# A second token tile's mixer work moved behind the first expert scores in a two-block fp32 kernel

## The chip, the cores and the metric

One core of one Trainium2 chip runs the whole program. The metric is the device time of one execution in microseconds (us). All data are fp32. The core has a matrix engine (TensorE, PE in the rows), a vector engine (VectorE, DVE), a scalar engine (ScalarE, ACT), GpSimd (POOL) and a sync engine (SP). SP issues plain DMAs on the hardware queue q1; POOL issues the gathers of expert rows on the software queue q0. Both queues run on the same 16 DMA engines.

## What is computed

Two blocks run one after the other on 256 tokens of width 1024. The change lies in the second, from the end of its mixer to the expert layer:

```python
o_hg = _rmsnorm_2(o, gn_w) * gate                 # linear attention, 4 heads of 128
y = jax.nn.gelu(y, approximate=False)             # state-space part
y = y * jax.nn.sigmoid(y @ w_glu + b_glu)         # "GLU"
mixed = jnp.concatenate([o_hg, o_s5], axis=-1) @ w_out[l]
x = x + gt1 * mixed
h2 = _rmsnorm_2(x, norm_ffn_w[l]) * (1.0 + sc2) + sh2
# _peer, per block of 128 tokens:
qh = (hb @ w_q).reshape(tb, PEER_HEADS, 2, PEER_HALF)          # 8 heads
s1, s2 = qh[:, :, 0] @ keys1.T, qh[:, :, 1] @ keys2.T          # 128 keys each
v1, i1 = lax.top_k(s1, 16); v2, i2 = lax.top_k(s2, 16)
best, pos = lax.top_k(v1[..., :, None] + v2[..., None, :], 16) # eidx from pos, i1, i2
gates = jax.nn.softmax(best)
act = jax.nn.gelu(jnp.einsum('td,thkd->thk', hb, u_tab[eidx]))
return jnp.einsum('thk,thkd->td', gates * act, v_tab[eidx])
```

After it comes `x + gt2 * peer` and a last RMSNorm. Each token picks 16 of 16,384 experts for each of 8 heads, and an expert has a row of 1024 in each of two tables.

## The kernel before

Tokens stand as two tiles of 128 (t = 0, 1). `mixer` (from L3119) holds the block's mixer, `projection_and_experts` (from L3607) what follows it; both write one program for each engine, run in order and tied by semaphores. No scheduler moves anything.

**End of the mixer.** PE reads the attention states of both tiles (L3373, L3380; `hg_out` counts tiles), multiplies the GLU weights by all 256 tokens (L3236, through `features(10, ...)`), turns the heads (L3395). ACT squares, roots and opens the GLU gate (L3595 to L3600), DVE scales the heads (L3523 to L3536), POOL multiplies by the gate (L3216).

**Output projection.** `out_tile(t, tile, k0, k1)` (L4084) multiplies one of 8 output tiles, `added` (L3946) adds the residual, `out_square` and `out_sum` (L4003, L4091) collect the norm, `inverted`, `out_root`, `out_scale`, `out_shift` (L3951, L4007, L3958, L4011) apply it.

**Queries and scores.** `PEER_QUERIES` lists 13 query steps: heads 0 to 4 for tile 0, heads 5 to 7 for both tiles, heads 0 to 4 for tile 1. `query_product` (L4107) multiplies a head's 1 MB of `peer_wq` by the tokens, `score` (L4124) the queries by the keys. `Search` (from L3667) finds the 16 experts on DVE; for the first unit (tile 0, head 0), `opening` (L3702) gives the first 8 and then the other 8, each told by `ranked`.

**Experts.** For each of 256 experts e (2 tiles, 8 heads, 16 each), POOL gathers 128 rows of 8 KB (L3848), one for each token: 1 MB. DVE takes the dot product (L3883), ACT makes a diagonal weight (L4042 to L4048), PE adds the weighted second half (L4186, `expert_done`). The ring has 8 buffers; gather e waits for expert e - 8. Buffers 4 to 7 lie in the weight ring and wait for the output products of tile 1 (`out_product`). Between experts PE does queries and scores of later heads. The weights of heads 0 and 1 are loaded by `early_loads`, of 2, 3, 5, 6, 4 and 7 by `sync`; a head waits for its whole group in `PEER_LOADS` = (0), (1), (2), (3, 5, 6, 4), (7).

## Time and profile before

| | us |
|---|---|
| median of 3 runs | 3091.54 (3090.03 to 3092.69) |
| profiled execution | 3085.72 |
| its span | 3083.9 |
| busy in the span: PE, DVE, ACT, POOL | 2921.8, 1841.9, 820.7, 575.8 |

A line of a timeline gives the start and the time of one or more instructions in us from the span's start, the engine, the line of the kernel, what is written from what, and the count; in brackets stands how long the engine was idle before it, and what ended that.
### The profile page before, as it was taken

Reading aid. Unit: us, or ns where it says so; the run is one execution under the profiler, and the core shown is the slowest. Engines: PE = TensorE matmul, PEld = TensorE weight load, DVE = VectorE, ACT = ScalarE, POOL = GpSimd, SP = SyncE. Lnnn points to the kernel's source line nnn. Section 1 sums busy time; section 2 is a strip of 40 time slices with the busy share of each in tenths; the row PEclk is TensorE's granted clock in tenths of the full one; section 3 lists DMA queues with packets and bytes.
Section 4 is the critical chain, followed back from the end, with each engine's and each line's share of the span. In section 5 each row is a group of like instructions: output and inputs, shape, how many; then the busy total and the mean of one; then the engine's idle time right before and its main releaser. Section 6 shows DMA issues by size and latency. Waiting matters only on the chain. (4 is left out here: it accounts for less than half of the span.)

```text
span 3083.9 us, 37671 instructions
## 1 busy us (share of the span) xinstructions
PE 2921.8 (95%) x14204; PEld 2256.3 (73%) x14204; DVE 1841.9 (60%) x3947; ACT 820.7 (27%) x1898; POOL 575.8 (19%) x561
## 2 busy tenths in 40 slices
PE   8999999999999999999999999999999999888777
PEld 3888877758888888887998878888887744443222
DVE  4556675367775677645345557534146677776774
ACT  2132344311002100012223430010033354444443
POOL 2223321010000000103112100000000344344342
PEclk8999999999999999999999999999999999999999
DMA  6212211154342443534222234569433899999997
GB/s 248 90 62 69 69 45 65 42 171 136 123 134 77 153 157 130 174 123 136 98 96 69 83 112 156 195 241 321 159 123 126 320 420 420 420 420 420 419 415 314
DMA packets 278068, 582.23 MB, mean 189 GB/s; under 512 B 11704, under 2 KB 228920, under 8 KB 241536
## 3 DMA queue, kind: packets, MB, share of 16 engines
q0 software_dynamic: 51504, 338.98, 27.6%
q1 hardware_dynamic: 226384, 240.84, 23.6%
q8 instruction: 114, 1.87, 0.2%
q14 instruction: 66, 0.54, 0.1%
HBM read 578.70 MB, written 1.08 MB: 188 GB/s over the span
## 5 line engine op out<-in xcount | busy, mean ns | idle before, releaser
L4186 PE MATMUL banks<-weight_ring,work 128*128 128x512 f32 x512 | 250.8, 614 | 56.7 <-ACT work L4048 55.9
L4186 PE MATMUL banks<-work 128*128 128x512 f32 x512 | 251.0, 613 | 40.1 <-ACT work L4048 36.6
L436 DVE CUSTOM_DVE_ANT_0 work<-work 128x1024 f32<-128x1024 f32 x176 | 210.0, 1227 | 95.0 <-ACT branches L2830 45.5
L2608 PE MATMUL banks<-normed,weight_ring 128*128 128x256 f32 x1088 | 237.1, 381 | 6.7 <-ACT normed L2808 3.8
L2608 PEld LDWEIGHTS banks<-normed,weight_ring 128*128 128x128 f32 x1088 | 207.6, 191 | 35.6 <-ACT normed L2808 4.2
L4186 PEld LDWEIGHTS banks<-weight_ring,work 128*128 128x128 f32 x512 | 88.1, 190 | 167.7 <-ACT work L4048 103.8
L3883 DVE CUSTOM_DVE_ANT_0 weight_ring<-weight_ring,branches 128x1024 f32<-128x1024 f32 x128 | 156.8, 1225 | 83.1 <-DMA weight_ring<-experts,branches 79.8
L3883 DVE CUSTOM_DVE_ANT_0 work<-work,branches 128x1024 f32<-128x1024 f32 x128 | 156.9, 1226 | 79.5 <-DMA work<-experts,branches 74.2
L4186 PEld LDWEIGHTS banks<-work 128*128 128x128 f32 x512 | 87.5, 189 | 153.5 <-ACT work L4048 88.4
L406 POOL DMA_DIRECT2D work<-ada_turned x96 | 51.0, 532 | 769.3 <-DVEq L442 769.3
L3848 POOL DMA_INDIRECT weight_ring<-experts,branches x128 | 138.8, 1084 | 192.3 <-PE banks L4186 187.8
L3848 POOL DMA_INDIRECT work<-experts,branches x128 | 132.9, 1038 | 208.8 <-PE banks L4186 168.9
L1944 PE MATMUL banks<-work 128*128 128x256 f32 x768 | 171.0, 379 | 0.0
L1944 PEld LDWEIGHTS banks<-work 128*128 128x128 f32 x768 | 145.9, 190 | 19.8
L2608 PE MATMUL banks<-branches,weight_ring 128*128 128x256 f32 x736 | 160.0, 379 | 0.0
L2608 PEld LDWEIGHTS banks<-branches,weight_ring 128*128 128x128 f32 x736 | 139.7, 190 | 18.9
L1361 POOL TENSOR_TENSOR branches<-weight_ring 128x512 f32<-128x512 f32 x40 | 51.4, 1284 | 529.7 <-DVE work L1580 142.0
L860 PE MATMUL banks<-normed,weight_ring 128*128 128x256 f32 (+1 forms) x512 | 137.0, 424 | 7.8 <-PEq L322 5.9
L4042 ACT ACTIVATE work<-work 128x1 f32<-128x1 f32 x256 | 52.2, 204 | 323.7 <-DVE work L3883 323.5
L860 PEld LDWEIGHTS banks<-normed,weight_ring 128*128 128x128 f32 x512 | 97.2, 191 | 46.5 <-issue 36.1
L1944 PE MATMUL banks<-normed,weight_ring 128*128 128x256 f32 x512 | 115.7, 379 | 0.0
L883 PE MATMUL banks<-branches 128*128 128x256 f32 x480 | 111.1, 380 | 0.0
(646 smaller groups left out, 5581.1 us busy)
## 6 DMA issues: line engine op xcount, KB each, us to landing
weight_ring<-w_in SPq DMA_DIRECT2D x98, 1024.0 KB, 5.0
weight_ring<-w_ffn_in SPq DMA_DIRECT2D x44, 1024.0 KB, 5.1
work<-ada_turned POOLq DMA_DIRECT2D x80, 512.0 KB, 3.6
work<-ada_turned POOLq DMA_DIRECT2D x16, 1536.0 KB, 9.0
weight_ring<-w_ffn_out SPq DMA_DIRECT2D x18, 1024.0 KB, 5.2
weight_ring<-w_out SPq DMA_DIRECT2D x12, 1024.0 KB, 5.2
weight_ring<-w_br_ml SPq DMA_DIRECT2D x8, 1024.0 KB, 5.1
weight_ring<-w_br_da SPq DMA_DIRECT2D x8, 1024.0 KB, 5.2
```

Of the source, the lines that this page charges most:

```text
L406: pool.dma_start(self.slots[n % ADA_SLOTS][:, 0:nt, :], self.a["ada_turned"][which, :, t0:t0 + nt, :]).then_inc(c.ada_loaded[n % ADA_SLOTS ...
L436: last = dve.tensor_tensor_reduce(out=out, in0=slot[:, t, :], in1=self.rows[:, row, :], scale=1.0, scalar=0.0, op0=ALU.mult, op1=ALU.add, ...
L860: last = pe.matmul(proj_bank(tile)[:, since:T], w[:, kk, half * P:(half + 1) * P], c.h[:, kk, since:T], start=kk == 0, stop=kk == KT - 1)
L883: last = pe.matmul(bank[:, half * NCTX:(half + 1) * NCTX], left[:, k], right[:, k], start=k == 0, stop=k == KT // 2 - 1)
L1361: pool.tensor_tensor(out[:, 0], part_of(w, 0, 1), part_of(w, 1, 1), ALU.add).then_inc(c.weights_mixed, 1)
L1944: last = pe.matmul(out[:, half * NCTX:(half + 1) * NCTX], left(k), right(k), start=k == 0, stop=k == KT // 2 - 1)
L2608: ins = pe.matmul(bank(i)[:, 0:NLAT], w[:, k - at, half * P:(half + 1) * P], source[:, k, lat], start=k == 0, stop=k == total - 1)
L3848: pool.indirect_dma_start(out=fetched[e % R], out_offset=None, in_=a["experts"], in_offset=bass.IndirectOffsetOnAxis(ap=experts_u[:, e:e + ...
L3883: dve.tensor_tensor_reduce(out=urows[e % R], in0=urows[e % R], in1=tokens[:, t, :], scale=1.0, scalar=0.0, op0=ALU.mult, op1=ALU.add, accu ...
L4042: act.activation(gl[:, r:r + 1], dot[:, at:at + 1], ACT.Gelu).then_inc(c.lifted, 1)
L4186: last = pe.matmul(c.banks[2 * t + half][:], diag[:, r, :], vrows[r][:, half * 512:(half + 1) * 512], start=e == t * H * K, stop=e == (t + ...
```

## The change

1. GLU, squares, root, head turning and gating are split by token tile. Tile 0's part stays; the reading of tile 1's states and the rest of its part go behind the scores of the first head. The GLU weights go to `big`, not to the ring, so that all four loads of `w_out` come earlier.
2. Each output tile of tile 0 is scaled by its gain as soon as the residual is added (`raise_tile`), with the shift as column 129. The first query is multiplied from these unnormed tokens (`raw_product`), and DVE and ACT multiply by 1/rms and add the shift's product afterwards.
3. On DVE, tile 1's heads stand inside `opening`; on POOL, tile 1's gating stands between gathers 1 and 2; on ACT, tile 1's squares, root and GLU stand between the shifts.
4. Head 4's weights are loaded early; head 7's go into two spent half buffers once tile 0's states are read; 2, 3, 5 and 6 are issued, as before, when both tiles' states are read. `PEER_LOADS` is unchanged.
5. Head 2's second half product goes behind experts 0 and 1. The store of tile 0's output waits for the last dot product.

```diff
-    FREED = (2, 4, 6, 8, 10, 12, 13, 14, 16, 18, 20, 22)
+    FREED = (2, 4, 6, 8, 10, 12, 13, 14, 16, 18)
+    OUT_ORDER, OUT_PIECES = (2, 3, 0, 1), (12, 13, 10, 11)
...
             loads = ([w_in[:, :, col + s * CHUNK:col + (s + 1) * CHUNK] for col in (0, 2 * HG_W, 3 * HG_W) for s in range(2)]
-                     + [glu[:, :, s * CHUNK:(s + 1) * CHUNK] for s in range(2)]
-                     + [w_out[:, :, s * CHUNK:(s + 1) * CHUNK] for s in range(D // CHUNK)])
+                     + [w_out[:, :, s * CHUNK:(s + 1) * CHUNK] for s in OUT_ORDER])
             for i, source in enumerate(loads, SLOTS):
-                if i == SLOTS + 10:
-                    sp.wait_ge(c.pe_out, INPUTS)
-                    sp.wait_ge(c.vec_out, STATES)
-                    rest.early_loads(sp)
+                if i == SLOTS + 9:
+                    sp.wait_ge(c.scored, HALF)
+                    sp.wait_ge(c.searched, 4)
+                    for s in range(2):
+                        sp.dma_start(glu_w[s], glu[:, :, s * CHUNK:(s + 1) * CHUNK]).then_inc(c.side_loaded, 16)
                 sp.wait_ge(c.product, FREED[i - SLOTS])
                 sp.dma_start(c.ring[:, i % SLOTS, 0:source.shape[1], :], source).then_inc(c.loaded[i % SLOTS], 16)
+            sp.wait_ge(c.pe_out, INPUTS)
+            sp.wait_ge(c.vec_out, STATES)
+            rest.early_loads(sp)
             rest.sync(sp)
 
...
+            def states_gated(t):
...
+                for tile in range(4):
+                    pool.wait_ge(c.merged, 4 * t + tile + 1)
+                    pool.tensor_tensor(out_s5[:, tile, its], y[:, tile, its], gate[:, tile, its], ALU.mult).then_inc(c.gated, 1)
...
-            for tile in range(4):
-                pool.wait_ge(c.merged, tile + 1)
-                pool.tensor_tensor(out_s5[:, tile], y[:, tile], gate[:, tile], ALU.mult).then_inc(c.gated, 1)
-            rest.gpsimd(pool)
+            states_gated(0)
+            rest.gpsimd(pool, states_gated)
...
-            features(10, lambda t: t % 2, wait_gated, y, 4)
-            for t in range(2):
+                    if h == H - 1:
+                        last.then_inc(c.hg_out, 1)
+                    yield
+
+            def glu_products(t):
+                for tile in range(4):
+                    w = glu_w[tile // 2]
+                    for k in range(4):
+                        last = pe.matmul(glu_place(t, tile), w[:, k, (tile % 2) * P:(tile % 2 + 1) * P],
+                                         y[:, k, t * P:(t + 1) * P], start=k == 0, stop=k == 3)
+                    if tile % 2:
+                        last.then_inc(c.product, 1)
+                    yield
+
+            def turn_heads(t):
                 pe.wait_ge(c.hg_scaled, t + 1)
...
+            for _ in states_read(0):
+                pass
+            assert next(gate, None) is None
+            pe.wait_ge(c.side_loaded, 32)
+            pe.wait_ge(c.powers, 4)
+            for _ in glu_products(0):
+                pass
+            turn_heads(0)
...
-    def gpsimd(pool):
+    def gpsimd(pool, states_gated):
         for e in range(2 * H * K):
+            if e == 0:
+                pool.wait_ge(c.hg_out, 2)
+            elif e == GATED_BEHIND:
+                pool.wait_ge(c.hg_turned, 2)
+                states_gated(1)
             if e % K == 0:
                 pool.wait_ge(c.ranked, e // K + 1 + (e > 0))
             elif e == K // 2:
@@ -3850,7 +3910,7 @@
...
+        def raise_tile(tile):
+            dve.wait_ge(c.out_added, tile + 1)
+            dve.tensor_scalar(raised[:, tile, 0:P], xs[:, tile, tokens_of(0)], c.modA[:, 0, tile:tile + 1], None, ALU.mult
+                              ).then_inc(c.scaled, 1)
+
+        def averaged_late():
+            heads_averaged(1)
+            for k in range(SCALES_FIRST, KT):
+                out_scale(0, k)
+            heads_scaled(1)
+
+        dve.tensor_copy(raised[:, :, P], c.mod[:, 3 * KT:4 * KT, 0]).then_inc(c.fed, 1)
+        dve.wait_ge(c.fed, 1)
         for tile in range(KT):
             added(0, tile)
+            raise_tile(tile)
...
+        dve.wait_ge(c.queried, 1)
+        dve.wait_ge(c.out_rooted, 1)
+        dve.tensor_copy(shift_q, raw_query[:, :, P]).then_inc(c.fed, 1)
+        dve.tensor_tensor(raw_q, raw_query[:, :, 0:P], out_rstd.unsqueeze(1).to_broadcast([P, 2, P]), ALU.mult).then_inc(c.fed, 1)
+        for k in range(SCALES_FIRST):
             out_scale(0, k)
         search = Search(dve, 0)
-        search.opening()
+        search.opening(averaged_late, lambda: heads_gated(1))
         for _ in search.weights(1):
...
+        act.wait_ge(c.fed, 3)
+        for i in range(2):
+            act.activation(qh[:, 0, i, 0:P], raw_q[:, i], ACT.Identity, bias=shift_q[:, i:i + 1]).then_inc(c.query_copied, 1)
+        for k in range(SHIFTS_FIRST):
             out_shift(0, k)
-        copy_query(0)
         copy_scores(0)
+        for k in range(SHIFTS_FIRST, SCALES_FIRST):
+            out_shift(0, k)
+        heads_squared(1)
+        heads_rooted(1)
+        for k in range(SCALES_FIRST, KT):
+            out_shift(0, k)
+        glu_opened(1)
+        act.wait_ge(c.hg_gated, 2)
         copy_tokens(0)
         exponentials(act, 1)
         copy_query(1)
         copy_scores(1)
+        act.wait_ge(c.gated, 8)
         for u, _ in units:
...
                 pe.wait_ge(c.out_shifted, k + 1)
             if i == 0 and k == 0 and n == PEER_BOTH:
                 pe.wait_ge(c.out_shifted, 2 * KT)
-            last = pe.matmul(query_bank(n)[:, i, first * P:end * P], wq_slots[head][:, k, i * P:(i + 1) * P],
...
+        def raw_product(k):
+            pe.wait_ge(c.scaled, k + 1)
+            for i in range(2):
+                last = pe.matmul(raw_query[:, i, :], wq_slots[0][:, k, i * P:(i + 1) * P], raised[:, k, :],
+                                 start=i == 0 and k == 0, stop=i == 1 and k == KT - 1)
...
+        pe.wait_ge(c.hg_gated, 1)
+        for first in (0, 4):
+            for tile in range(first, first + 4):
+                if first:
+                    pe.wait_ge(c.out_added, tile - 3)
+                out_tile(0, tile, 0, 4)
+                if tile in (4, 5):
+                    out_sum(0, tile - 2)
+            if first == 0:
+                pe.wait_ge(c.gated, 4)
+            for tile in range(first, first + 4):
+                out_tile(0, tile, 4, 8)
+                if tile % 4 >= 2:
+                    out_sum(0, tile - 2)
+        pe.wait_ge(c.wq_loaded[0], 32)
+        for k in range(4):
+            raw_product(k)
+        out_sum(0, 6)
+        raw_product(4)
+        raw_product(5)
+        out_sum(0, 7)
+        raw_product(6)
+        raw_product(7)
+        next(states_read)
+        score(0)
+        for _ in chain(states_read, glu_products):
+            pass
+        turn_heads()
+        pe.wait_ge(c.out_shifted, KT)
+        turn_tokens(0)
+        query(1)
         pe.wait_ge(c.hg_gated, 2)
-        for tile in range(KT):
-            out_tile(0, tile, 0, 4)
-        pe.wait_ge(c.gated, 4)
-        for tile in range(KT):
-            out_tile(0, tile, 4, 8)
-            if tile >= 2:
-                out_sum(0, tile - 2)
-        pe.wait_ge(c.out_added, 2)
-        out_tile(1, 0, 0, 4)
-        out_sum(0, 6)
-        out_tile(1, 0, 4, 5)
-        out_sum(0, 7)
-        out_tile(1, 0, 5, 8)
-        out_tile(1, 1, 0, 8)
-        query(0)
-        turn_tokens(0)
-        score(0)
+        pe.wait_ge(c.gated, 8)
+        for tile in range(2):
+            out_tile(1, tile, 0, 8)
+        score(1)
         for tile in range(2, KT):
+            if tile == 4:
+                pe.wait_ge(c.token_copied, 2)
             out_tile(1, tile, 0, 8)
-        query(1)
...
+                if u == 0 and at < 2:
+                    for k in range(4 * at, 4 * at + 4):
+                        query_product(2, 1, k)
                 if PEER_AHEAD + u < len(PEER_QUERIES):
                     query_product(PEER_AHEAD + u, at // KT, at % KT)
...
     def early_loads(sp):
         sp.dma_start(keys, a["keys"]).then_inc(c.wq_loaded[0], 16)
-        load(sp, 0)
-        load(sp, 1)
+        for head in (0, 1, 4):
+            load(sp, head)
 
     def sync(sp):
+        sp.wait_ge(c.hg_out, 1)
+        for i in range(2):
+            sp.dma_start(wq_halves[i], wq[:, 4 * i:4 * i + 4, 7 * CHUNK:8 * CHUNK]).then_inc(c.wq_loaded[load_of(7)], 16)
         sp.wait_ge(c.hg_out, 2)
         for head in (2, 3, 5, 6):
             load(sp, head)
-        sp.wait_ge(c.gated, 4)
-        load(sp, 4)
-        sp.wait_ge(c.out_product, 2 * KT)
-        load(sp, 7)
         sp.wait_ge(c.finished, 6)
+        sp.wait_ge(c.dotted, 2 * H * K)
         sp.dma_start(out_rows[0:P, :], tokens[:, 0, :]).then_inc(c.stored, 16)
```

On SP, the loads of query weights (`peer_wq`) and the first store. `hg_out` is waited for at 1 and then at 2 after the change. Before:

```order
L4211 DMA merged<-peer_wq 128x8x256
L3206 DMA weight_ring<-w_out 128x8x256 [waits product] x2
L4211 DMA work<-peer_wq 128x8x256 [waits hg_out]
L4211 DMA work<-peer_wq 128x8x256
L4211 DMA branches<-peer_wq 128x8x256
L4211 DMA constants_sb<-peer_wq 128x8x256
L4211 DMA normed<-peer_wq 128x8x256 [waits gated]
L4211 DMA merged<-peer_wq 128x8x256 [waits out_product]
L4227 DMA out<-branches 128x1024 [waits finished]
```

After:

```order
L4328 DMA merged<-peer_wq 128x8x256
L4328 DMA normed<-peer_wq 128x8x256
L4338 DMA branches<-peer_wq 128x4x256 [waits hg_out]
L4338 DMA work<-peer_wq 128x4x256
L4328 DMA work<-peer_wq 128x8x256 [waits hg_out]
L4328 DMA work<-peer_wq 128x8x256
L4328 DMA branches<-peer_wq 128x8x256
L4328 DMA constants_sb<-peer_wq 128x8x256
L4344 DMA out<-branches 128x1024 [waits dotted,finished]
```

The wait on `out_product` is gone; four loads (heads 2, 3, 5, 6) stand behind the second `hg_out`, which PE now raises later.

On PE, around the first head's scores (L4124, now L4222). Before:

```order
L4107 MATMUL banks<-normed,stream 128x128 [waits out_shifted,wq_loaded0]
L4107 MATMUL banks<-normed,stream 128x128 [waits out_shifted] x7
L4107 MATMUL banks<-normed,stream 128x128 x8
L4132 MATMUL banks<-constants_sb,normed 128x128 x8
L4124 MATMUL banks<-branches 128x128 [waits query_copied]
L4124 MATMUL banks<-branches 128x128
L4084 MATMUL banks<-merged,weight_ring 128x128 [waits loaded1]
```

After, with tile 1's states (L3388, L3395) around the scores:

```order
L4205 MATMUL banks<-branches,stream 128x129 [waits scaled]
L4205 MATMUL banks<-branches,stream 128x129
L3388 MATMUL banks<-work 128x128
L3395 MATMUL banks<-work 32x128 x2
L3395 MATMUL banks<-branches,work 32x128 x2
L4222 MATMUL banks<-branches 128x128 [waits query_copied]
L4222 MATMUL banks<-branches 128x128
L3388 MATMUL banks<-work 128x128
L3395 MATMUL banks<-work 32x128 x2
```

The scores stand ahead of all output products of tile 1, and three of its four heads of states behind them.

On PE, the last products ahead of the experts and experts 0 to 2 (L4186, now L4300). Before:

```order
L4107 MATMUL banks<-normed,work 128x128 [waits query_copied,wq_loaded2]
L4107 MATMUL banks<-normed,work 128x128 x7
L4124 MATMUL banks<-branches 128x128 [waits query_copied]
L4124 MATMUL banks<-branches 128x128
L4107 MATMUL banks<-normed,work 128x128 x8
L4186 MATMUL banks<-work 128x512 [waits gathered0,weighted,token_copied]
L4186 MATMUL banks<-work 128x512
L4107 MATMUL banks<-normed,work 128x128 [waits query_copied,wq_loaded3]
L4186 MATMUL banks<-work 128x512 [waits gathered1,weighted]
L4186 MATMUL banks<-work 128x512
L4107 MATMUL banks<-normed,work 128x128
```

After:

```order
L4197 MATMUL banks<-normed,work 128x128 [waits query_copied,wq_loaded2]
L4197 MATMUL banks<-normed,work 128x128 x7
L4300 MATMUL banks<-work 128x512 [waits gathered0,weighted,token_copied]
L4300 MATMUL banks<-work 128x512
L4197 MATMUL banks<-normed,work 128x128 x4
L4197 MATMUL banks<-normed,work 128x128 [waits query_copied,wq_loaded3]
L4300 MATMUL banks<-work 128x512 [waits gathered1,weighted]
L4300 MATMUL banks<-work 128x512
L4197 MATMUL banks<-normed,work 128x128 x5
L4300 MATMUL banks<-work 128x512 [waits gathered2,weighted]
L4300 MATMUL banks<-work 128x512
L4197 MATMUL banks<-normed,work 128x128
```

The wait for the group of heads 3, 5, 6, 4 (`wq_loaded3`) stands behind expert 0 in both.

## Rows read from the trace of the kernel before

**Rows 1.** The page: the span in 40 slices of 77.1 us, DMA busy tenths and GB/s.

```profile
DMA  6212211154342443534222234569433899999997
GB/s 248 90 62 69 69 45 65 42 171 136 123 134 77 153 157 130 174 123 136 98 96 69 83 112 156 195 241 321 159 123 126 320 420 420 420 420 420 419 415 314
```

**Rows 2.** Stretches: us, busy us of each engine (x instructions), clock, DMA share, GB/s.

```profile
2404.00:2416.00 12.00, 11.83 (x103) 11.67 (x102) 6.51 (x35) 5.81 (x14) 0.95 (x1) 1.00 0.00 1
2416.00:2420.00 4.00, 4.00 (x39) 4.00 (x38) 3.68 (x17) 0.22 (x1) 2.92 (x4) 1.00 0.81 276
2444.00:2446.00 2.00, 2.00 (x4) 0.92 (x3) 1.90 (x6) 1.70 (x7) 0.00 (x0) 0.50 1.01 404
2480.00:3060.00 580.00, 492.03 (x1292) 218.76 (x1292) 406.92 (x1024) 264.18 (x774) 241.46 (x229) 1.00 1.01 419
3064.00:3072.00 8.00, 6.48 (x14) 2.22 (x13) 4.22 (x7) 2.72 (x9) 0.00 (x0) 1.00 0.06 26
```

**Rows 3.** DMA queues from 2388 to 2400 us: packets, MB, share.

```profile
q1 hardware_dynamic: 4141, 4.18, 109.1%
```

**Rows 4.** DMA queues from 2430 to 2446 us.

```profile
q0 software_dynamic: 793, 5.73, 87.1%
q1 hardware_dynamic: 794, 0.81, 14.6%
```

**Rows 5.** DMA queues from 2785 to 2800 us, where tile 0's output is stored.

```profile
q1 hardware_dynamic: 144, 0.52, 8.6%
```

**Rows 6.** Timeline, SP issuing DMAs: start us, us, queue, line, what.

```profile
2368.22 0.50 SPq L4214 DMA_DIRECT2D branches<-keys  x1
...
2383.24 1.67 SPq L4211 DMA_DIRECT2D work<-peer_wq  x2
...
2425.32 0.37 SPq L4211 DMA_DIRECT2D merged<-peer_wq  x1
```

**Rows 7.** Timeline, TensorE: start, us, line, out<-in, shapes, count.

```profile
2371.82 0.49 PE L3373 MATMUL banks<-work 128*128 128x128 f32 x2
...
2374.92 3.72 PE L3236 MATMUL banks<-branches,weight_ring 128*128 128x256 f32 x16
...
2385.38 10.06 PE L4084 MATMUL banks<-merged,weight_ring 128*128 128x128 f32 x88 [1.70 <-DVE merged L3536]
...
2410.84 10.88 PE L4084 MATMUL banks<-merged,weight_ring 128*128 128x128 f32 x96
...
2431.24 1.96 PE L4186 MATMUL banks<-work 128*128 128x512 f32 x4 [1.01 <-issue]
...
2443.04 3.60 PE L4186 MATMUL banks<-weight_ring,work 128*128 128x512 f32 x4 [3.35 <-ACT work L4048]
...
2446.69 1.88 PE L4186 MATMUL banks<-weight_ring,work 128*128 128x512 f32 x4
```

**Rows 8.** Timeline, the other engines, up to the first gathers.

```profile
2375.67 1.28 ACT L3597 ACT_TABLE_LOAD   x1
...
2376.97 0.21 ACT L3597 ACTIVATE work<-work 128x8 f32<-128x8 f32 x1
...
2402.85 0.29 DVE L3951 TENSOR_SCALAR branches<-banks 128x128 f32<-128x128 f32 x1 [1.44 <-PE banks L4091]
...
2404.16 0.31 ACT L4007 ACTIVATE branches<-branches 128x128 f32<-128x128 f32 x1 [2.40 <-DVE branches L3953]
...
2411.45 0.49 DVE L3707 MAX8 work<-branches 128x8 f32<-128x128 f32 x2 [4.76 <-ACT branches L3987]
...
2415.05 1.02 POOL L3848 DMA_INDIRECT work<-experts,branches  x1 [30.94 <-DVEq L3764]
...
2433.99 0.93 POOL L3848 DMA_INDIRECT work<-experts,branches  x1 [6.24 <-PE banks L4186]
```

**Rows 9.** Timeline, the last dot product and the last store.

```profile
3071.24 1.22 DVE L3883 CUSTOM_DVE_ANT_0 weight_ring<-weight_ring,branches 128x1024 f32<-128x1024 f32 x1 [1.26 <-DMA weight_ring<-experts,branches]
...
3079.76 1.00 SPq L4231 DMA_DIRECT2D out<-branches  x2
```

More of the change, by code:

```diff
@@ L3519, in _, with heads_averaged @@
             dve.sem_inc(c.vec_out, 1)
-            for t in range(2):
+            def heads_averaged(t):
+                part = slice(4 * t, 4 * t + 4)
                 dve.wait_ge(c.squared, t + 1)
-                chain.mark(dve.tensor_reduce(power[:, 4 * t:4 * t + 4], token_squares[:, t].rearrange("p (h v) -> p h v", h=H), AX.X,
-                                             ALU.add))
-            chain.wait()
-            chain(dve.tensor_scalar(power, power, 1.0 / P, EPS, ALU.mult, ALU.add))
@@ L3592, in _, with heads_squared, heads_rooted, glu_opened @@
                 act.activation(g[:, tile, :], gate_bank(tile), ACT.Silu).then_inc(c.cleared, 1)
[L3593 removed]
+            def heads_squared(t):
                 act.wait_ge(c.hg_out, t + 1)
                 act.activation(token_squares[:, t], c.banks[4 + t], ACT.Square).then_inc(c.squared, 1)
[L3596 to L3602 removed]
+            def heads_rooted(t):
+                part = slice(4 * t, 4 * t + 4)
+                act.wait_ge(c.inverted, t + 1)
+                act.activation(token_rstd[:, part], power[:, part], ACT.Sqrt).then_inc(c.rooted, 1)
+            def glu_opened(t):
+                its = slice(t * P, (t + 1) * P)
+                for tile in range(4):
+                    act.wait_ge(c.product, GLU_TILES + (4 if t else tile // 2 + 1))
+                    act.activation(gate[:, tile, its], glu_place(t, tile), ACT.Sigmoid,
+                                   bias=c.vector("glu_b", tile, tile + 1)).then_inc(c.merged, 1)
+            heads_squared(0)
+            heads_rooted(0)
+            glu_opened(0)
+            rest.scalar(act, heads_squared, heads_rooted, glu_opened)
 Programs = namedtuple("Programs", "early_loads sync gpsimd tensor vector scalar")
```

110 lines of the change are left out of this document (59 added, 51 removed).

## The prediction

> **What bounds the kernel now.** The page's slices come first [rows 1]: from slice 33 to 39 the DMA engines are at 9 tenths and move 420 GB/s. Until about 2416 us they are free now and then, behind it never. The table of stretches says the same [rows 2]: DMA share 1.01 and 419 GB/s over 580 us, while PE, DVE and ACT have room. One gather is 128 rows of 8 KB, 1.049 MB, so 2.50 us at 419 GB/s, and 256 gathers are 640 us. The last dot product starts at 3071.24 on its transfer [rows 9], and the span ends some 12.7 us later. The moving of data starts 2.3 us after the first gather's issue at 2415.05 [rows 8]: 4 us at 276 of 419 GB/s are 2.6 us of moving, so 2417.4 [rows 2]. From there to 3071.2 are 653.8 us: 640 for the gathers, 3.0 for a load of query weights, 1.25 for a store (both below), and 9.6 more, which show as one engine of the 16 that runs behind (share 0.06 from 3064 to 3072 [rows 2]). So the end is set by three things: when DMA work begins for good, how many bytes lie behind that point, and how long DMA stands idle in it. An earlier first gather alone is worth nothing if other bytes move behind it.
>
> **The change, before the first gather.** Tile 0's states are done at 2371.82 and tile 1's at 2374.92 [rows 7]; the latter's 3.1 us go. GLU took 32 instructions of 256 columns in two runs of 3.72 [rows 7]; for one tile it is 32 of 128 columns at 0.113 (96 in 10.88 [rows 7]), 3.6, until 2375.4. From the last GLU product at 2382.8 to the first output product at 2385.38 both tiles' turning and gating took 2.6; for one tile I take 1.7. Output products start at 2377.1 instead of 2385.38. Squares, root and gate on ACT, with two table loads of 1.28, end about 2376.8, just ahead. Behind that, before: 77 products of two instructions to the last sum at 2402.85 [rows 7, 8]. After: 64 output products, 8 sums and 12 of the 16 raw query products, 84 times 0.227, 19.1, so 2396.2. The raw products cost PE nothing new (they replace `query(0)`), but 2.7 us of them now stand ahead of the norm, where 1.1 of tile 1's stood. DVE's eight `raise_tile` stand between `added` of the last tile and its sum by some 0.3 each; PE is the slower of the two, so only the last counts, and that is hidden by raw products 0 to 3.
>
> From the last sum to the first search DVE took 8.6 (2402.85 to 2411.45 [rows 8]): mean, reciprocal and root 1.66, then scales, shifts and query on PE. Now behind the root: scale and bias of a 256-column query 1.3, scores 0.6, copy and the queue of three shifts 0.8, or 4.4 in all. Search at 2400.6, first gather 3.6 behind it as now [rows 8]: 2404.2, 10.8 us earlier.
>
> The second tile's states end (one head ahead of the scores, three behind at 0.78 each) near 2402.4. That raises the second `hg_out`, for the gather and for SP.
>
> **The change, bytes.** Before, seven of the eight loads of query weights were issued from 2368 on and landed by 2402, with DMA idle behind them (0.00 from 2404 to 2416 [rows 2, 6]). Only head 7's was issued at 2425.32, among gathers [rows 6]. Now heads 0, 1, 4 and 7 land in the free stretch, but heads 2, 3, 5 and 6 are issued at 2402.4. A load alone moves at 4.18 MB in 12 us [rows 3]: 3.0 us for its 1.049 MB. Among gathers its cost in engine time is the same (0.81 MB of loads and 5.73 MB of gathers in 16 us [rows 4]: 13.7 us of gathers leave 2.3 for 0.81 MB, 2.9 per load). So:
> - DMA work begins at 2403.9 (issue, then 1.5; I take less than the gather's 2.3, which is the bound) instead of 2417.4: -13.5.
> - Four loads behind that point: +12.0. Head 7's gone from it: -3.0.
> - The late store: 0.52 MB at 419 GB/s [rows 5]: -1.25. It runs behind the last dot, when DMA is idle, and has 7 us before the last store at 3079.76 [rows 9]: nothing there.
>
> Without idle time that is -5.7.
>
> **The change, idle time: a new wait.** PE waits for the group of heads 3, 5, 6 and 4 right behind expert 0. Before, it had long landed. Now I follow it. PE ends tile 1's part: GLU and turning to 2406.9, token turning and `query(1)` to 2411.9, eight output tiles of 1.83 and score to 2427.1, half of head 2 to 2429.1 (tile 1's states and GLU moved in here, 7 us, use up what was won ahead). Expert 0 ends at 2430.9 and gather 8 is issued; before, that was at 2433.99 [rows 8]. Then four products of head 2, and at 2431.9 PE stands at the group. Have the four loads landed? The work from 2403.9 is 12.0 plus gathers 0 to 8, 22.5: it ends at 2438.4 in whatever order. Gathers and loads take turns packet by packet: 793 of 8 KB against 794 of 1 KB [rows 4], so a load gets an eighth of the gathers' bytes. Before the first gather moves (2406.5) the loads get 0.9 MB, between gathers that come late (2 and 3 behind tile 1's gating on POOL, 4 to 7 behind output products) some 1.1 MB more, with nine gathers 0.14 MB each; the last 0.9 MB go alone behind gather 8. The last load lands near 2439, 7 us after PE wants it. Queued behind PE's wait are experts 1 to 8, and behind `expert_done` POOL's gathers 9 on. When the group lands, all gathers issued have landed too, so DMA is idle until PE has done expert 1.
>
> That costs: PE stood still, and 3.35 us of idle time before expert 4 were enough for the clock at 0.50 and 3.60 us instead of 1.88 [rows 2, 7]. So 0.3 + 3.6 + 0.2 for POOL + 2.3 to data: 6.4. Then ACT's copy of head 2's query, which now needs the four products behind expert 1, stands ahead of expert 2's weight; the next gather comes late by 2.0. Sum +8.4 (bounds: 4 when the clock stays up and the copy hides, 11 when expert 2 is slow too). I take 7.2, since the trailing engine uses 1 to 2 us of the gap to catch up.
>
> **The sum.** -5.7 + 7.2 = +1.5. Against the profiled 3085.72 that is 3087.2; by the median of the runs, 5.8 higher, 3093.0.
>
> At one place a rule of the Trainium skill bears on this. The rows show packets of both queues one for one. "DMA: Bandwidth & Descriptors", section "Queues, rings and completion order", states that an engine "round-robins between the queue rows it has work for, at packet granularity" and takes about 9 to 17 descriptors for a packet. By that rule, if only the loads were bundled so and the gathers' rows went singly, a load would get more bytes than the gathers, the group would land near 2420, and the time would be the first rival's. The one-for-one counts speak against it.
>
> **Rivals.**
> *The loads land in time* (no wait, or one under 1 us). It needs them to get about 1.2 MB more before 2432, by larger turns or later gathers. For it: POOL holds back gathers 2 to 7, and I may have them too early. Against: the work left is 6.5 us too much, in any order. Time: -5.7, 3085.9.
> *PE stays slow behind the wait.* Place: experts 1 to 8, when all eight buffers have landed. At 0.50 an expert with its query product takes 3.9 us against 2.50 of DMA, so each of seven more starves DMA by 1.4, 9.8 in all: 3102.8. Against: behind the wait before expert 4, full speed was back after one pair of experts (1.88 at 2446.69 [rows 7]). It decides if the clock stays down for more than four experts.
> *The front part is not won.* If the raw query is held up (its product starts late, or score and shifts queue on ACT), `hg_out` and the loads come up to 4 us later, with the same wait behind: 3097.
>
> **How the numbers follow.** Chances: forecast 0.62, with its own range 3089 to 3097; loads in time 0.18; slow PE 0.08; front not won 0.12. A measurement can tell about 0.2%, 6.2 us, so from 3085.4 to 3097.7 it is the same. Of loads in time, half comes out under that, with 0.03 of the forecast: faster 0.12. Slow PE and a third of the last: slower 0.12. Same 0.76. The range 3085.5 to 3098.5 leaves out the slow PE and half of the first rival.
>
> **What would show it.** Right: first gather issued near 2404 and search at 2401; DMA busy from 2404 to 2438 with queue q1 in it until the end, then a hole of 5 to 8 us; PE idle from 2432 to 2439 with `peer_wq` as its releaser, a clock of 0.50 behind it; 419 GB/s with no store in it later; last dot within 3 us of 3071. Wrong: no hole (then the first rival), a hole of over 12 us, or DMA idle between 2404 and 2432.

## The result, and the profile of the changed kernel

The changed kernel takes 3095.15 us (median of 20 executions, 3091.51 to 3100.05), the kernel before 3091.52 (20, 3087.39 to 3094.70). The ratio is 1.0014, with a 95% interval from 1.0008 to 1.0021. By the bound of 0.2% that is the same time. The forecast was 3093.0, 1.5 above the kernel before; measured are 3.6, and the interval of the ratio, 2.5 to 6.5 us, leaves out the 1.5. Two executions of those below were slow, one of a_q2 (4339 us) and one of the kernel before (3170), and the ratios leave them out.

**One point in both traces.** The profiled executions differ by 9.4 us (3095.08 and 3085.72), and almost half of that lies ahead of the changed code. Each fence below has ScalarE's first block copy behind the decays, in code that no edit touches (first kernel before, then changed), and of the changed kernel also the last dot product and the stores:

```profile
2364.76 1.15 ACT L3586 ACTIVATE work<-banks 32x128 f32<-32x128 f32 x4 [4.93 <-PE banks L3321]
```

```profile
2369.23 1.14 ACT L3617 ACTIVATE work<-banks 32x128 f32<-32x128 f32 x4 [4.93 <-PE banks L3336]
...
3080.61 1.23 DVE L3943 CUSTOM_DVE_ANT_0 weight_ring<-weight_ring,branches 128x1024 f32<-128x1024 f32 x1 [1.26 <-DMA weight_ring<-experts,branches]
...
3081.92 0.36 SPq L4344 DMA_DIRECT2D out<-branches  x1
3089.12 0.99 SPq L4348 DMA_DIRECT2D out<-branches  x2
```

From this copy to the last dot product it is 706.5 us before (3071.24 in [rows 9]) and 711.4 after: 4.9 more by the traces (one trace of each kernel). From here on "from the copy" means this distance, and times of the changed kernel less 4.47 can be held against the forecast's. (The expectations below call the copy, loosely, the first instruction of the second token tile's GLU.)

**Where the DMA engines stand idle.** Stretches of the changed kernel, columns as in [rows 2]: us, busy us of PE, PEld, DVE, ACT and POOL with their instructions, granted clock, DMA share, GB/s.

```profile
2404.00:2408.00 4.00, 4.00 (x48) 3.04 (x47) 3.42 (x20) 2.24 (x7) 0.00 (x0) 1.00 0.08 17
2408.00:2416.00 8.00, 7.78 (x71) 7.59 (x70) 7.50 (x31) 6.18 (x13) 5.42 (x8) 1.00 1.04 357
2416.00:2436.00 20.00, 18.71 (x157) 17.57 (x155) 14.47 (x46) 3.46 (x8) 5.20 (x6) 1.00 1.02 402
2436.00:2440.00 4.00, 0.00 (x0) 0.00 (x0) 2.52 (x7) 0.00 (x0) 0.00 (x0) 0.61 1.06 415
2440.00:2444.00 4.00, 0.00 (x0) 0.00 (x0) 3.58 (x10) 0.00 (x0) 0.00 (x0) 0.50 0.67 262
2444.00:2448.00 4.00, 3.32 (x6) 1.77 (x7) 1.09 (x2) 0.00 (x0) 0.00 (x0) 0.50 0.00 1
2448.00:2452.00 4.00, 2.91 (x13) 2.21 (x11) 0.00 (x0) 1.27 (x6) 0.94 (x1) 0.69 0.30 82
2452.00:2456.00 4.00, 4.00 (x13) 2.09 (x14) 0.51 (x3) 3.88 (x7) 0.94 (x1) 1.00 0.51 195
2456.00:2460.00 4.00, 3.94 (x15) 2.07 (x14) 2.18 (x5) 3.71 (x15) 1.87 (x2) 1.00 0.94 354
2490.00:3070.00 580.00, 492.92 (x1292) 219.13 (x1292) 407.89 (x1027) 263.45 (x776) 240.34 (x229) 1.00 1.01 420
```

DMA work begins at 2407.6, and the engines are full until 2440. Then they stop, and are busy again only from 2460 on. From 2490 it is as before, with 420 GB/s.

**What stops them.** TensorE in the changed kernel: expert 0, half of head 2, the wait, expert 1 at half clock; then expert 2, which waits for ScalarE.

```profile
2431.94 1.88 PE L4300 MATMUL banks<-work 128*128 128x512 f32 x4
2433.66 1.05 PE L4197 MATMUL banks<-normed,work 128*128 128x128 f32 x8
2444.68 0.80 PE L4197 MATMUL banks<-normed,work 128*128 128x128 f32 x2 [9.97 <-DMA constants_sb<-peer_wq]
2445.27 3.62 PE L4300 MATMUL banks<-work 128*128 128x512 f32 x4
2448.68 2.15 PE L4197 MATMUL banks<-normed,work 128*128 128x128 f32 x10
2451.92 1.98 PE L4300 MATMUL banks<-work 128*128 128x512 f32 x4 [1.09 <-ACT work L4126]
```

The releaser `constants_sb<-peer_wq` is head 6's load, the last of the four that SP issues from 2406.54 on. GpSimd's gathers show what hangs on it: gather 8 at 2434.61, just behind expert 0, and gather 9 only after 13.6 us of idle time.

```profile
2408.99 1.02 POOL L3908 DMA_INDIRECT work<-experts,branches  x1 [26.94 <-DVEq L3819]
...
2434.61 0.94 POOL L3908 DMA_INDIRECT work<-experts,branches  x1 [1.83 <-PE banks L4300]
2449.16 0.94 POOL L3908 DMA_INDIRECT work<-experts,branches  x1 [13.61 <-PE banks L4300]
2454.18 0.94 POOL L3908 DMA_INDIRECT work<-experts,branches  x1 [4.08 <-PE banks L4300]
2456.12 0.94 POOL L3908 DMA_INDIRECT work<-experts,branches  x1 [1.00 <-PE banks L4300]
```

Each load is reported by the 16 DMA engines one by one (of some loads the trace lacks reports; of heads 3 and 6 it has all 16). In the trace of the changed kernel head 3's reports come from 2414.3 to 2418.3, head 6's from 2442.8 to 2444.64, and at 2444.68 TensorE moves. The product behind expert 0 is one of head 3. So TensorE waits for 10 us for data it does not use yet, because `PEER_LOADS` counts 3, 5, 6 and 4 with one semaphore.

### The profile page after: what moved, and what is told of

Its sections match the earlier page's. It is cut to its first block and busy times, and to the rows that moved or that the text cites. A ratio compares the mean times of both kernels' runs of the same rounds, so it can differ in the third digit from the quotient of the medians.

```text
span 3093.3 us, 37774 instructions
## 1 busy us (share of the span) xinstructions
PE 2925.3 (95%) x14236; PEld 2261.2 (73%) x14236; DVE 1845.0 (60%) x3960; ACT 819.9 (27%) x1905; POOL 572.6 (19%) x565
## 5 line engine op out<-in xcount | busy, mean ns | idle before, releaser
L4300 PE MATMUL banks<-weight_ring,work 128*128 128x512 f32 x512 | 249.3, 611 | 51.1 <-ACT work L4126 50.0
L4300 PE MATMUL banks<-work 128*128 128x512 f32 x512 | 252.5, 616 | 40.3 <-ACT work L4126 39.3
L4300 PEld LDWEIGHTS banks<-weight_ring,work 128*128 128x128 f32 x512 | 87.6, 189 | 161.9 <-ACT work L4126 99.3
L4300 PEld LDWEIGHTS banks<-work 128*128 128x128 f32 x512 | 88.2, 190 | 153.4 <-ACT work L4126 90.7
```

The lines of the kernel that those rows point to most:

```text
L4300: last = pe.matmul(c.banks[2 * t + half][:], diag[:, r, :], vrows[r][:, half * 512:(half + 1) * 512], start=e == t * H * K, stop=e == (t + ...
```

## The experiments

**Theory.** The forecast's sum: an earlier start of DMA work and its bytes give -5.7, and the group wait, by the idle DMA time it makes, gives it back. **Rivals.** The added work or the order in which the queues share the engines costs the time and the wait only covers it; or the start of the gathers decides.

Each table row below is from one kernel: its median and the ratio to the kernel before on the same chip with its 95% interval; from the copy to the last dot product in its trace; and how many us the DMA engines lost in the 70 us behind the first gathered packet (the sum, over stretches of 1 us, of what the packets started in it lack of 415 GB/s). In b_late, b_late_split and a_hold this packet itself comes later than in the kernel that was edited, by 2.9, 2.9 and 10.6 us; the last column does not count that.

| kernel | median, us | ratio | copy to last dot | DMA lost |
|---|---|---|---|---|
| before | 3090.5 to 3091.5 | 1 | 706.5 | 2.0 |
| b_split | 3090.60 | 0.9999 (0.9990 to 1.0008) | 706.1 | 1.9 |
| changed | 3095.15 | 1.0014 (1.0008 to 1.0021) | 711.4 | 13.4 |
| a_again | 3094.56 | 1.0011 (1.0002 to 1.0020) | 711.6 | 13.2 |
| a_split | 3084.54 | 0.9984 (0.9976 to 0.9993) | 700.7 | 1.2 |
| a_split_q2 | 3084.65 | 0.9979 (0.9970 to 0.9988) | 700.7 | 1.2 |
| a_split_store | 3088.36 | 0.9986 (0.9977 to 0.9995) | 701.6 | 1.3 |
| a_hold | 3097.66 | 1.0023 (1.0013 to 1.0032) | 711.6 | 8.1 |
| a_hold_two | 3087.91 | 0.9990 (0.9981 to 0.9999) | 704.2 | 6.0 |
| a_busy | 3091.59 | 1.0002 (0.9993 to 1.0011) | 708.1 | 10.1 |
| a_q2 | 3094.86 | 1.0015 (1.0005 to 1.0024) | 706.3 | 8.3 |
| a_q2_again | 3094.97 | 1.0008 (0.9999 to 1.0018) | 709.3 | 10.9 |
| b_late | 3107.10 | 1.0050 (1.0036 to 1.0063) | 719.9 | 8.1 |
| b_late_split | 3102.01 | 1.0037 (1.0023 to 1.0051) | 717.0 | 1.3 |

### The group wait alone: a_split, and b_split as its control

```diff
-PEER_LOADS = ((0,), (1,), (2,), (3, 5, 6, 4), (7,))
+PEER_LOADS = ((0,), (1, 4), (2,), (3,), (5, 6, 7))
...
-                pe.wait_ge(c.wq_loaded[group], 16 * (len(PEER_LOADS[group]) + (head in (0, 7))))
+                pe.wait_ge(c.wq_loaded[group], 16 * (len(PEER_LOADS[group]) + (group in (0, 4))))
```

> The changed kernel with head 3's query weights counted by a semaphore of their own, instead of one that also waits for heads 5 and 6 (head 4 shares head 1's, head 7 the one of 5 and 6). Nothing moves in any queue. In the changed kernel's trace the second of the four late loads, head 3's, has landed at 2415.5 us, and TensorE stands from 2434.7 to 2444.7 for the fourth. Theory (the wait for a load that it does not need makes the hole in the DMA work and the slow clock behind it): no wait behind expert 0, the granted clock stays at 1.00, no slice of the DMA engines under 0.9 from 2440 to 2448; the time falls by the idle time of the sum, 7 to 10 us, to 3085 to 3088 (before: 3091.5). Rival (what was added to ScalarE and VectorE, or the order in which the transfers share the engines, costs the time, and the wait only covers it): 3094 to 3096. Rival two (the second gap, behind the copy of head 2's query, takes its place): 3089 to 3092.

Head 3's last report in the changed kernel is at 2418.3, not at 2415.5; it is early enough either way.

Measured: 3084.54, 10.0 to 10.6 us under the changed kernel and 6.0 under the kernel before; from the copy to the last dot 10.7 less. TensorE runs through, and so do the DMA engines. TensorE of a_split at experts 0 to 2, then its stretches:

```profile
2428.47 1.88 PE L4300 MATMUL banks<-work 128*128 128x512 f32 x4
2430.19 1.28 PE L4197 MATMUL banks<-normed,work 128*128 128x128 f32 x10
2431.31 1.88 PE L4300 MATMUL banks<-work 128*128 128x512 f32 x4
2433.03 1.28 PE L4197 MATMUL banks<-normed,work 128*128 128x128 f32 x10
2435.41 1.98 PE L4300 MATMUL banks<-work 128*128 128x512 f32 x4 [1.10 <-ACT work L4126]
```

```profile
2436.00:2440.00 4.00, 4.00 (x16) 2.13 (x14) 3.12 (x8) 3.88 (x8) 1.48 (x2) 1.00 1.02 411
2440.00:2444.00 4.00, 3.94 (x12) 2.03 (x13) 3.68 (x12) 3.63 (x15) 1.56 (x2) 1.00 1.04 421
2444.00:2448.00 4.00, 4.00 (x15) 2.09 (x15) 3.89 (x18) 1.72 (x7) 2.92 (x2) 1.00 1.01 419
```

Only which loads share a semaphore differs; no load, gather or product moves in its queue. So the wait is the cause, and the first rival falls. Rival two falls as well: the second gap keeps 1.10 us of TensorE's time, and no DMA time. The same edit in the kernel before, whose loads have long landed:

```diff
-PEER_LOADS = ((0,), (1,), (2,), (3, 5, 6, 4), (7,))
+PEER_LOADS = ((0, 1), (2,), (3,), (5, 6, 4), (7,))
```

> The kernel before with head 3's query weights counted by a semaphore of their own (heads 0 and 1 share one). Its loads land at 2391 to 2397 us, 34 us and more ahead of expert 0. Theory (the split is worth something only where the group's last load is late): 3090.5, within 1 us of the kernel before. Rival (a smaller group helps by itself, by fewer waits of TensorE among the experts): 3 us less or more, 3087.5 or lower.

Measured: 3090.60 beside 3091.13, as expected. The split by itself is worth nothing that shows (ratio 0.9990 to 1.0008).

### The changed kernel once more: a_again

> The changed kernel once more, as it stands, beside the three others of this call, since the executions of one kernel lie 5 to 10 us apart and its first measurement was made apart from the experiments. Theory: 3.6 to 4.9 us over the kernel before (3.6 by the medians, 4.9 by the two traces counted from the first instruction of the second token tile's GLU): 3094 to 3096. Rival (the difference was the chip's): within 2 us of the kernel before.

Measured: 3094.56, 3.4 over the kernel before, and from the copy 711.6, beside 711.4 the first time. The difference is the kernel's, not the chip's.

### The same bytes in another order: a_hold and a_hold_two

```diff
             if e == 0:
                 pool.wait_ge(c.hg_out, 2)
+                pool.wait_ge(c.wq_loaded[3], 64)
```

> The changed kernel with GpSimd's first gather held until all four late loads have landed, so the same bytes go in another order and the group wait of TensorE is over before it is reached. The loads alone went at 349 GB/s in the kernel before: 4.19 MB in 12.0 us from 2407.9 us of the profiled changed kernel, so the first gather starts near 2420 to 2422 and lands with the seven behind it by 2440, while TensorE reaches expert 0 at 2432. Theory (idle DMA time is what counts): no wait of 10 us in TensorE; lost are 2.0 us by the lower rate of the loads and 2 to 3 us between the last load's landing and the first gather's data, gained 7 to 10 of idle time: 3089 to 3092. Rival (the gathers' start decides, whatever stands idle later): 12 us later start, 3100 or more.

Measured: 3097.66, outside the theory's range and short of the rival's. Its trace says why: TensorE stands for 11 us, but ahead of the second token tile's output products (L4174), not behind expert 0. GpSimd waits at gather 0, and the second tile's gating (L3228) is queued behind it. GpSimd and TensorE of a_hold:

```profile
2425.88 1.02 POOL L3909 DMA_INDIRECT work<-experts,branches  x1 [40.48 <-DMA constants_sb<-peer_wq]
2427.20 0.97 POOL L3909 DMA_INDIRECT work<-experts,branches  x1 [0.30 <-issue]
2428.18 1.70 POOL L3228 TENSOR_TENSOR merged<-branches,work 128x128 f32<-128x128 f32 x4
```

```profile
2429.98 5.52 PE L4174 MATMUL banks<-merged,weight_ring 128*128 128x128 f32 x32 [11.06 <-issue]
```

I had overlooked that, so the run can't tell theory from rival. a_hold_two puts the wait ahead of gather 2, behind the gating:

```diff
+            if e == 2:
+                pool.wait_ge(c.wq_loaded[3], 64)
             if e >= R:
```

> The changed kernel with its group wait kept, and GpSimd's third gather held until the four late loads have landed. Unlike in a_hold (3097.7 us), where GpSimd stood in front of the second token tile's gating and so stopped TensorE for 11 us, the first two gathers and that gating go ahead. The same bytes, 4.19 MB of loads and 2.10 MB of gathers, should be in by 2423 to 2425 us at 380 to 400 GB/s, the third gather's data start 2 to 3 us behind, and TensorE reaches expert 0 at 2432 with the group wait met. Theory (what counts is how long the DMA engines idle, and the load that lands last): 3087 to 3090, TensorE without a DMA wait. Rival (delaying gathers costs what it delays): 3095 or more.

Measured: 3087.91, inside the theory's range, though from the copy gather 2 is issued 13 us later than in the changed kernel and gather 7 still 1.7. TensorE finds the whole group landed. So a gather held back does not cost what it is held back by; the delay costs no more than the DMA time that it leaves idle. Gathers 0 and 1 start here as in the changed kernel: what a later first gather would cost by itself no run shows. 4.8 us more than in a_split are lost, and the last dot is 3.5 later.

### The clock behind the wait: a_busy

The edit adds products whose result is not used; it leaves nothing out.

```diff
                 last.then_inc(c.expert_done, 1)
+                if u == 0 and at == 0:
+                    pe.wait_ge(c.score_copied, 2)
+                    for _ in range(40):
+                        pe.matmul(c.banks[5][:, 0:P], c.constant("ident"), c.constant("ident"), start=True, stop=True)
```

> The changed kernel with 40 products of the identity with itself (into a free bank, results not used) that TensorE does once while it waits for the loads behind expert 0. Theory: expert 1 and the products behind the wait run at the full clock, 1.9 instead of 3.6 us for expert 1, the hole before it stays; 1.5 to 3 us less than the changed kernel, 3092 to 3093.6. Rival (the hole alone costs, and the slow clock hides behind transfers in flight): 3095.

Measured: 3091.59, 3.0 to 3.6 us under the changed kernel (3.3 from the copy). The wait ends at the same landing, 0.3 us sooner from the copy. But expert 1 takes 1.88, and expert 2 starts 4.4 us behind the release instead of 7.2:

```profile
2445.77 0.49 PE L4197 MATMUL banks<-normed,work 128*128 128x128 f32 x2 [0.69 <-DMA constants_sb<-peer_wq]
2446.10 1.88 PE L4300 MATMUL banks<-work 128*128 128x512 f32 x4
2447.82 1.28 PE L4197 MATMUL banks<-normed,work 128*128 128x128 f32 x10
2450.20 1.98 PE L4300 MATMUL banks<-work 128*128 128x512 f32 x4 [1.10 <-ACT work L4126]
```

So the granted clock of 0.50 (1.2 GHz) behind the standstill is worth some 3 of the 10.7 us.

### The second gap: a_q2, a_q2_again, a_split_q2

```diff
-        for k in range(KT):
-            query_product(2, 0, k)
+        for i in range(2):
+            for k in range(KT):
+                query_product(2, i, k)
...
-                if u == 0 and at < 2:
-                    for k in range(4 * at, 4 * at + 4):
-                        query_product(2, 1, k)
```

> The changed kernel with the second half of head 2's query products ahead of expert 0 again, as in the kernel before, instead of between experts 0 and 1. Theory: the copy of head 2's query is then made before the wait for the loads, ScalarE is free for expert 2's weight and the second gap (DMA engines 0.30 to 0.51 busy at 2448 to 2456) goes, 2 to 3 us: 3092.3 to 3093.3; the stop behind expert 0 stays and ends at the same landing. Rival (the second gap is only the echo of the first: slots free late because experts 1 to 3 run late): 3095. If expert 0, 1.8 us later, frees the first slot so late that the first hole grows: 3096 to 3097.

> a_q2 once more (both halves of head 2's query products ahead of expert 0), beside the changed kernel. Its trace had the second gap gone and the last dot 5.1 us sooner than the changed kernel's, counted from the same instruction of the GLU, while the medians were equal and its executions spread from 3087 to 3102 us. Theory one (the trace is right, the median was unlucky): 3 to 5 us less than a_again, 3090 to 3092. Theory two (with TensorE stopped behind expert 0 in the same way, the clock comes back at different times and eats the gain): equal to a_again within 1.5 us and again a wider spread.

Measured: 3094.86 and 3094.97, by the medians no gain; from the copy 5.1 and 2.0 us less than the changed kernel. In the first trace the load lands early (wait until 2439.62, 73.2 from the copy, where the changed kernel has 75.5); in the second it ends at 75.7, 0.2 later than there, and only the second gap is gone. Less what the end of the wait moved, the second gap is worth 2.9 and 2.3 us. The executions spread by 14.7 and 9.1 us, the changed kernel's by 8.5 and 6.2. The traces speak for 2 us, the medians for under 1; which holds stays open.

> The changed kernel with head 3's weights counted apart (as in a_split, 3084.5 us) and with both halves of head 2's query products ahead of expert 0. In the trace of a_split the DMA engines are busy throughout from 2408 us, no slice under 1.00. Theory (with the DMA engines never idle nothing on TensorE or ScalarE counts any more): the same time as a_split, 3083 to 3086. Rival (the copy of head 2's query ahead of the weights of expert 2 still costs 1.1 us there, TensorE's gap ahead of expert 2 in a_split): 1 to 2 us less than a_split, 3082.5 to 3083.5. If expert 0, 1.8 us later, empties the ring of slots: 3086 to 3087.

Measured: 3084.65 beside a_split's 3084.54, and 700.7 from the copy for both. With DMA never idle, TensorE's gap of 1.1 us costs nothing.

### The store: a_split_store

```diff
         sp.wait_ge(c.finished, 6)
-        sp.wait_ge(c.dotted, 2 * H * K)
         sp.dma_start(out_rows[0:P, :], tokens[:, 0, :]).then_inc(c.stored, 16)
```

> a_split (3084.5 us) with the wait of the store of the first token tile for the last dot taken out, so that its 0.52 MB go among the gathers again, as in the kernel before. Theory (DMA engines busy to the end: bytes count): 1.25 us more by the rate of 419 GB/s, 3085.8, and 1.2 to 1.3 us more from the first GLU instruction to the last dot. Rival (the end of the program, with three stores behind the last dot instead of two, gives the same back): 3084.5 at an earlier end behind the last dot.

Measured: from the copy 0.8 us more; by the ratios (0.9984 and 0.9986) 0.6, by the medians beside the kernel before 3.2, with intervals of some 2.8 us on either side. The times can't tell the 1.25 from nothing, and the 0.8 is from one trace of each. The rival's other half is answered: from the last dot product to the end of the span it is 12.7 us in both, so the third store behind the last dot costs nothing.

### The wait made in the kernel before: b_late and b_late_split

```diff
-        sp.wait_ge(c.hg_out, 2)
-        for head in (2, 3, 5, 6):
-            load(sp, head)
         sp.wait_ge(c.gated, 4)
         load(sp, 4)
+        sp.wait_ge(c.score_copied, 1)
+        for head in (2, 3, 5, 6):
+            load(sp, head)
```

> The kernel before with the loads of the query weights of heads 2, 3, 5 and 6 issued not during the token statistics (2388 to 2400 us of its trace) but behind the first scores, some 6 us ahead of the first gather; TensorE's program and its group wait are those of the kernel before. Theory: the loads have 6 us alone (2.1 MB), the other half goes by turns with the gathers, descriptor by descriptor, 1 KB against 8 KB, and lands at 2441 to 2446; TensorE waits there behind expert 0 for 8 to 12 us at half clock behind it: 5 to 6 us for the bytes and 8 to 11 us for idle DMA engines, 3103 to 3108. Rival (the group wait is harmless in this order): 3095 to 3097.

Measured: 3107.10. TensorE of b_late behind expert 0:

```profile
2457.58 0.80 PE L4107 MATMUL banks<-normed,work 128*128 128x128 f32 x2 [15.75 <-DMA constants_sb<-peer_wq]
2458.17 3.27 PE L4186 MATMUL banks<-work 128*128 128x512 f32 x4
```

The time is as expected, the wait longer than the 8 to 12 us. The expected parts, 5 to 6 us for the bytes and 8 to 11 of idle time, came out otherwise: of the 13.4 us from the copy 7.3 are start and bytes (as in b_late_split, below), and 6.1 is what the DMA engines lost more than in the kernel before. That the total fits is in part luck. b_late_split also has `PEER_LOADS = ((0,), (1,), (2,), (3,), (4, 5, 6, 7))`:

> As b_late, with head 3's weights counted by a semaphore of their own (4, 5, 6 and 7 share one). Theory: no wait behind expert 0, no hole; left are the bytes behind the gathers' start, 5 to 6 us: 3095 to 3097, 8 to 11 us less than b_late. Rival (late loads cost by themselves, through the order in which the queues share the engines): 3101 or more.

Measured: 3102.01, which is the rival's time. But not by its mechanism. Behind expert 0 there is no wait. It comes at expert 16, where head 4 is due: my own grouping makes it wait for head 7's load, issued last. TensorE and the stretches of b_late_split there:

```profile
2493.03 0.80 PE L4107 MATMUL banks<-normed 128*128 128x128 f32 x2 [7.62 <-DMA merged<-peer_wq]
```

```profile
2504.00:2508.00 4.00, 2.21 (x6) 1.06 (x6) 3.80 (x9) 3.88 (x7) 1.37 (x2) 1.00 0.95 363
2508.00:2512.00 4.00, 3.50 (x13) 2.07 (x14) 0.86 (x4) 2.66 (x10) 0.94 (x1) 1.00 0.83 289
2512.00:2516.00 4.00, 4.00 (x14) 1.93 (x13) 3.93 (x13) 1.19 (x4) 2.53 (x2) 1.00 0.94 301
2516.00:2520.00 4.00, 4.00 (x13) 2.08 (x12) 3.93 (x16) 2.38 (x8) 2.61 (x3) 1.00 0.94 369
```

Against 420 GB/s these four lack 16 x (1 - 330.5 / 420), 3.4 us, where the 330.5 is their mean. The rest of its 10.5 us from the copy: the first gather's data 2.9 later (its issue is as early as before; the loads stand ahead of it on the engines) and 1.86 MB more behind that point, 4.4. That makes 10.7. So of the rival's mechanism, the order on shared engines, 2.9 us are there. A control meant to be free of the fault had it at another place.

## Why the prediction was right, and where its sizes were off

**The front part: right.** Times of the changed kernel less 4.47, forecast in brackets: last sum read by DVE 2396.2 (2396.2), search 2400.3 (2400.6), first gather issued 2404.5 (2404.2), SP's loads 2402.1 (2402.4). TensorE reached expert 0 at 2427.5, 1.6 ahead of the forecast's 2429.1, which only made it wait longer. The third rival (front part not won) fell. What came otherwise is the order on the engines: the first gathered packet moves at 2409.2, where the forecast had 2406.5, and by then 1.9 MB of the loads have moved, not 0.9. The last landing did not come sooner for it, as the forecast's sum of the work, "in whatever order", said.

**Bytes and start, -5.7: right.** a_split is that sum without idle time: 5.8 under the kernel before from the copy, 6.0 by the medians. By parts: the first gathered packet moves 7.6 us earlier (44.4 from the copy, before 52.0), and behind it 2.28 MB of loads instead of 1.57 MB of a load and a store, 1.7 us; -5.9.

**The wait: right in place, cause and end.** The group did not land in time (first rival), and the clock was back by expert 2 (second rival: seven slow experts; expert 2 takes 1.98). The last load was reported by most engines at 2438.6 and by the last at 2440.2 in the forecast's time, which had 2439.

**One reading of the rows was wrong, without effect.** The forecast took the 793 packets of the software queue in [rows 4] as rows of 8 KB. The same view counts 93 packets under 512 B in that stretch; the 8 KB rows are 700. The bytes that the sum uses are right.

**The term that was mis-sized is the idle time, taken at +7.2.** Measured are 10.7 from the copy (changed less a_split). It was 8.4 of idle time, less 1.2 that the trailing engine would catch up. Idle were some 12 (12.2 in the table, changed less a_split; 8.7, 2.7 and 1.0 by stretches):

- *The first hole, 6.4.* The chain itself came out as summed: from the release at 2444.68 to gather 9 at 2449.16 are 4.5 us (forecast 4.1), and 2.0 to its data (82 GB/s from 2448 to 2452 are 0.8 us of moving, so from 2451.2; forecast 2.3). From the last report to there are 6.6. But the forecast's hole began with the last landing. The group counts all 16 engines, so the wait ends with the trailing one, and the others stood idle before. The stretches from 2440 to 2452 lack 8.7 us of 415 GB/s, so 2.1 more than the chain. Stretches of 1 us of the changed kernel show the others stop while a few finish:

```profile
2442.00:2443.00 1.00, 0.00 (x0) 0.00 (x0) 0.93 (x3) 0.00 (x0) 0.00 (x0) 0.50 0.55 192
2443.00:2444.00 1.00, 0.00 (x0) 0.00 (x0) 0.79 (x5) 0.00 (x0) 0.00 (x0) 0.50 0.15 52
2444.00:2445.00 1.00, 0.32 (x1) 0.32 (x2) 1.00 (x1) 0.00 (x0) 0.00 (x0) 0.50 0.01 4
```
- *The second gap, 2.0.* The stretches from 2452 to 2460 lack 2.7 us, and those from 2460 to 2468, at 367 and 363 GB/s, 1.0. Gather 10 is issued 5.0 us behind gather 9, where 2.5 would keep the engines busy. The sum priced the half clock for expert 1 alone, 1.7 us; but the ten query products behind it, for which ScalarE's copy waits, ran at half clock in part too (2.15 us, in a_busy 1.28). Taking the gap away was worth 2.3 and 2.9 in a_q2's traces, so the gap was near its forecast, and the rest is the slow filling behind the hole.
- *The 1.2 taken off.* The changed kernel lost 12.2 us more than a_split and ended 10.7 later, so 1.5 came back. For a_hold_two, a_busy and both a_q2 the table gives 1.1 to 1.5. The size was right. That it is the trailing engine that catches up is not shown: the traces do not tell one engine's packets from another's.

So the term fell 3.5 us short, and about 2 of them are the engines that had finished while the last one had not. The forecast took off what the trailing engine catches up, and did not add what the others lose while they wait for it. The mechanism was right. By the forecast's own signs two were missed: a hole of 5 to 8 us (8.7 to 2452) and the last dot within 3 us of 3071 (3076.1 in its time). What the sum did not ask is which of the four loads head 3 needs; the remedy was in the same line of the kernel.

**What remains between the two ways of counting.** By the traces the change costs 4.9 us, by the medians 3.6 and 3.4. The last section shows that executions differ by more than that ahead of the copy.

## What to carry to other kernels

When loads are moved late, look at what each wait counts, not only at when the data it needs arrives: a semaphore shared by a group turns the last load of the group into the price of the first. Here two lines of grouping were worth 10.7 us and turned a kernel 0.14% slower into one 0.16% faster, and a careless regrouping made the same kind of wait elsewhere. Where DMA bounds the end, price an edit by start, bytes and idle DMA time, and count as idle also the time in which a wait for a whole load leaves the engines that have finished without work, and the slow clock behind a stop.

## What the runs showed of the hardware

**The clock dips of the unchanged part come in sets.** The 5 to 10 us between executions that lie ahead of the copy go with short stretches of lower granted clock in code that no edit touches. Stretches of 50 us of the kernel before, then of a_split, then of the changed kernel:

```profile
600.00:650.00 50.00, 46.41 (x156) 29.10 (x155) 26.10 (x47) 14.43 (x26) 4.47 (x8) 1.00 0.31 106
1800.00:1850.00 50.00, 45.51 (x236) 40.27 (x235) 35.13 (x126) 14.81 (x31) 3.13 (x5) 1.00 0.35 115
```

```profile
600.00:650.00 50.00, 46.41 (x158) 29.58 (x157) 23.55 (x42) 14.53 (x27) 3.95 (x7) 1.00 0.31 106
1800.00:1850.00 50.00, 45.07 (x232) 39.92 (x233) 34.10 (x124) 15.84 (x32) 3.14 (x5) 1.00 0.36 118
```

```profile
600.00:650.00 50.00, 46.41 (x154) 29.48 (x153) 23.73 (x42) 14.70 (x27) 3.94 (x7) 0.97 0.30 105
1800.00:1850.00 50.00, 45.04 (x228) 39.39 (x227) 32.55 (x122) 16.03 (x32) 3.13 (x5) 0.97 0.36 121
```

The first two, whose clock stays at 1.00 in both stretches, reach the copy at 2364.8 and 2365.8; the changed kernel (also 0.97 from 1400 to 1450) at 2369.2, a_hold at 2372.6 and b_late_split at 2374.5, both with 0.93 at 600 and 0.97 at 1800. a_q2 and a_q2_again are one kernel: the first has 1.00 in both stretches and reaches the copy at 2366.4, the second 0.93 and 0.97 and reaches it at 2374.9, so 8.5 of the 11.6 us between these two executions lie ahead of the copy. What picks the set is open. To tell 1 us, count from a point behind them.

**A shared engine gives packets, not bytes.** While both queues had work in the changed kernel (2430 to 2434 us), 188 packets of the gathers (172 rows of 8 KB and 16 of 4 bytes) passed beside 190 of the loads (189 rows of 1 KB). [rows 4] has 793 beside 794. Heads 5 and 6, two loads that would take 6 us alone ([rows 3] by the load), lasted 26 (last reports 2418.3 to 2444.6).
